# Last convolution taps moved into the first attention, top-k rounds placed between index sums, GpSimd held back behind ropes, fewer idle matmuls

## The reference

```
first_block:  x += 0.5*swiglu(rms_norm(x))                      # ffn0
              q, k, v, u, mq = rms_norm(x) @ w_in               # mixer A
              y = [sliding_window_attention(q,k,v,sinks),       # 8 heads, window 128
                   silu(layer_norm(causal_conv31(glu(u)))),     # 256 channels, 31 taps
                   memory_cross_attention(mq, mem)]             # 4 heads, 256 keys
              x += y @ w_out;  x += 0.5*swiglu(rms_norm(x))     # ffn1
second_block: mod = silu(c) @ ada_w + ada_b                     # shifts, scales, gates
  mixer B:    q, k, v, qi, ki, wi = h @ w_in
              score = sum over 8 index heads of relu(qi.ki)*wi  # causal
              keep the 128 highest scores of each query (top-k)
              o = softmax over the kept keys, 16 heads; x += g1*(o @ w_out)
              x += g2*swiglu(h)                                 # ffn2
  mixer C:    (b * causal_conv3(c*u)) @ w_out, then ffn3
```

## Time and profile before

| | us |
|---|---|
| runs of the kernel | 2164.49, 2162.81, 2172.12 (median 2164.49) |
| the profiled execution | 2165.37, of which the span from first to last instruction is 2163.4 |
| PE busy, PE weight loads | 2135.3, 1758.0 |
| DVE busy, ACT busy, POOL busy | 1211.7, 783.2, 233.8 |
| mean granted TensorE clock | 0.994 of full |

### The profile page before, as it was taken

The page is one execution under the profiler, slowest core; times in us unless marked ns, Lnnn a source line. Parts: engine busy times, 40 slices in busy tenths (PEclk is TensorE's granted clock), DMA queues, the critical chain, the costliest instruction groups (busy, mean ns, idle before and its releaser), DMA issues.

```text
span 2163.4 us, 28943 instructions
## 1 busy us (share of the span) xinstructions
PE 2135.3 (99%) x10238; PEld 1758.0 (81%) x10238; DVE 1211.7 (56%) x1760; ACT 783.2 (36%) x1081; POOL 233.8 (11%) x237
## 2 busy tenths in 40 slices
PE   9999999999999999999989999999999999999999
PEld 8888888877888888877767888888888878888887
DVE  7555444886566554465796575554456456333333
ACT  6222333547442223334355342223333234222222
POOL 0000201650200030014300200000000000000000
PEclk9999999999999999999989999999999999999999
DMA  5555333320345542323300245542332222222232
GB/s 190 183 185 184 104 95 109 124 82 2 107 156 184 187 136 83 93 93 113 107 21 1 85 139 185 185 155 74 101 117 90 95 88 89 96 97 97 78 99 85
DMA packets 75733, 242.96 MB, mean 112 GB/s; under 512 B 9328, under 2 KB 9584, under 8 KB 75536
## 3 DMA queue, kind: packets, MB, share of 16 engines
q1 hardware_dynamic: 61376, 189.61, 26.9%
q0 software_dynamic: 14288, 52.44, 7.8%
HBM read 235.65 MB, written 2.10 MB: 110 GB/s over the span
## 4 chain that ended last, share of the span: by engine, by line
PE 89%; DVE 8%; ACT 1%; issue 1%; DMA 0%; SPq 0%; ACTq 0%; DVEq 0%
PE ps L675 27%; PE ps L677 27%; PE ps L676 27%; PE ps L993 2%; DVE ps L1931 2%; PE ps L951 1%; PE ps L972 1%; PE ps L770 1%; DVE tmp L1604 1%; DVE score L2032 1%; DVE top L2030 1%; PE ps L954 1%; PE ps L1119 0%; DVE w_lo L1561 0%; DVE ropB L1805 0%
## 5 line engine op out<-in xcount | busy, mean ns | idle before, releaser
L675 PE MATMUL ps<-h_hi,w_hi 128*128 128x512 f32 x1888 | 743.3, 394 | 1.3 <-DVE h_lo L1871 0.9
L677 PE MATMUL ps<-h_hi,w_lo 128*128 128x512 f32 x1888 | 735.8, 390 | 0.0
L676 PE MATMUL ps<-h_lo,w_hi 128*128 128x512 f32 x1888 | 735.3, 389 | 0.0
L1561 DVE TENSOR_TENSOR w_lo<-w_raw,w_hi 128x1024 fp32r<-128x1024 f32 x336 | 412.8, 1230 | 433.3 <-ACT w_hi L1202 418.3
L1202 ACT ACTIVATE w_hi<-w_raw 128x1024 fp32r<-128x1024 f32 x383 | 402.3, 1051 | 247.0 <-PE ps L677 245.5
L675 PEld LDWEIGHTS ps<-h_hi,w_hi 128*128 128x128 f32 x1888 | 354.0, 187 | 81.0 <-issue 7.1
L677 PEld LDWEIGHTS ps<-h_hi,w_lo 128*128 128x128 f32 x1888 | 353.8, 187 | 76.2
L676 PEld LDWEIGHTS ps<-h_lo,w_hi 128*128 128x128 f32 x1888 | 354.1, 188 | 72.7 <-issue 0.2
L675 PE MATMUL ps<-hid_hi,w_hi 128*128 128x512 f32 x704 | 273.9, 389 | 0.0
L676 PE MATMUL ps<-hid_lo,w_hi 128*128 128x512 f32 x704 | 273.9, 389 | 0.0
L677 PE MATMUL ps<-hid_hi,w_lo 128*128 128x512 f32 x704 | 273.9, 389 | 0.0
(11 more groups left out here) (304 smaller groups left out, 1749.1 us busy)
## 6 DMA issues: line engine op xcount, KB each, us to landing
ada_raw<-in_ada_w POOLq DMA_DIRECT2D x96, 512.0 KB, 4.3
w_raw<-in_gate SPq DMA_DIRECT2D x88, 512.0 KB, 3.5
w_raw<-in_up SPq DMA_DIRECT2D x88, 512.0 KB, 3.5
w_raw<-in_down SPq DMA_DIRECT2D x64, 384.0 KB, 3.0
w_raw<-in_down SPq DMA_DIRECT2D x64, 320.0 KB, 2.8
w_raw<-in_w_mix_c SPq DMA_DIRECT2D x24, 512.0 KB, 3.5
w_raw<-in_w_mix_b SPq DMA_DIRECT2D x17, 512.0 KB, 3.5
w_raw<-in_w_mix SPq DMA_DIRECT2D x16, 512.0 KB, 3.5
```

The source lines that it names most:

```text
L675: pe.matmul(dest, s_hi, m_hi, start=first and n == 0, stop=False)
L676: pe.matmul(dest, s_hi, m_lo, start=False, stop=False)
L677: mm = pe.matmul(dest, s_lo, m_hi, start=False, stop=last and n == len(pairs) - 1)
L1561: dve.tensor_tensor(chunk(w_lo, slot, WT), chunk(w_raw, slot, WT), f32(chunk(w_hi, slot, WT)), ALU.subtract).then_inc(w_lo_done, 1)
```

## The change

In mixer A, 11 of the 62 taps go from steps 13 to 15 into turns 1 to 11 of the first attention, one a turn, all of half 1. Tap 19 of that half now writes `conv` and taps 20 to 30 read and write it in SBUF; the score of pair 1, which uses banks 2 and 3, waits for tap 19. The total moves to u = 13, the two centrings to u = 15 and 16, the squares to 16 and 17, the sums to u = 20 to 23. In mixer B each step has rounds ahead of its index sums and between their two halves, 33 in all; the 15 left come at u = 7 to 21, and qB7 is roped at u = 1. GpSimd's split of job 9 waits for the rope of qi3, of job 10 and 11 for index sums, and of jobs 15 to 20 for the ropes of qB0 to qB5. The idle matmuls are 4 in the first attention and 5 in the second.

```diff
--- before.py
+++ after.py
@@ -424,9 +424,12 @@
             TOPS += [(b, "tri")] + [(b, r, s) for r in range(ROUNDS) for s in ("max", "take")] + [(b, "mask")]
         top = Marks(sem("top"), TOPS)
         ROUND_LIST = [(b, r) for b in range(1, TT) for r in range(ROUNDS)]
-        TOPS_AT = {9: 3, 10: 3, 11: 2, 12: 3, 13: 3, 14: 3, 15: 3, 16: 3, 17: 2}
-        TOP_EARLY = sum(TOPS_AT.values())
-        TAPS_AT = {2: 3, 3: 3, 4: 6, 5: 6, 6: 5, 7: 6, 8: 3, 9: 5, 10: 5, 11: 5, 12: 4, 13: 4, 14: 4, 15: 3}
+        TOPS_AT = {8: (0, 1), 9: (4, 1), 10: (5, 2), 11: (4, 1), 12: (0, 2), 13: (3, 0), 14: (3, 0), 15: (3, 0), 16: (3, 0),
+                   17: (1, 0)}
+        TOP_EARLY = sum(before + between for before, between in TOPS_AT.values())
+        TAPS_AT = {2: 3, 3: 3, 4: 6, 5: 6, 6: 5, 7: 6, 8: 3, 9: 5, 10: 5, 11: 5, 12: 4}
+        LATE_TAPS = 2 * CONV_A - sum(TAPS_AT.values())
+        LEAVES_BANK = [CONV_A - 1, CONV_A - LATE_TAPS - 1]
 
         def index_slot(m, part):
 
@@ -660,6 +663,14 @@
             pool.wait_ge(x_done, 32)
             pool.dma_start(matsB[:, :], A["mats"]).then_inc(stage_in, 16)
             for j in range(LEAD, len(TILES_B) + KC):
+                if j == 9:
+                    after(pool, h_roped, "qi3")
+                if j == 10:
+                    after(pool, i_sum, (1, 5))
+                if j == 11:
+                    after(pool, i_sum, (2, 1))
+                if 15 <= j <= 20:
+                    after(pool, h_roped, f"qB{j - 15}")
                 split(first_job["mixB"] + j)
             after(pool, h_roped, "qB7")
             ada_steps(2)
@@ -924,12 +935,12 @@
                                        start=True, stop=True)
                 mm.then_inc(h_spread.at(t), 1)
 
-            def attention(pairs, score, turn, values, sums, std):
+            def attention(pairs, score, turn, values, sums, std, beside_exp):
                 for u in range(len(pairs) + 5):
                     if u == 2:
                         after(pe, a_misc, std)
                         after(pe, u_score, pairs[1])
-                        idle(10)
+                        idle(beside_exp)
                     if u < len(pairs):
                         score(pairs[u])
                     if 2 <= u < len(pairs) + 2:
@@ -1041,13 +1052,13 @@
             betweenA(len(TILES_A), 0)
 
             def sumsA(u):
-                if u == 2:
+                if u == LATE_TAPS + 2:
                     after(pe, d_conv, (CONV_A - 1, 1))
                     for c in range(2):
                         mm = pe.matmul(bank(5), ones[:, :], chunk(conv, c), start=c == 0, stop=c == 1)
                     mm.then_inc(p_misc.at("conv_total"), 1)
-                if 5 <= u < 5 + TT:
-                    b = u - 5
+                if LATE_TAPS + 9 <= u < LATE_TAPS + 9 + TT:
+                    b = u - LATE_TAPS - 9
                     if b == 0:
                         after(pe, a_misc, "conv_sq1")
                     for c in range(2):
@@ -1069,7 +1080,7 @@
             def scoreA(pair):
                 kind, j, b = pair
                 if PAIRS_A.index(pair) == 1:
-                    after(pe, d_conv, (CONV_A - 1, 1))
+                    after(pe, d_conv, (LEAVES_BANK[1], 1))
                 if b == 0 and kind == "win":
                     after(pe, h_roped, f"qA{j}")
                 if b == 0 and kind == "mem":
@@ -1094,7 +1105,7 @@
                                                                (2 * (j * MT + q) + half + 1) * HV] for q in range(MT)])
 
             take(first_job["outA"] + 1)
-            attention(PAIRS_A, scoreA, lambda pair: pair_turn(pair, pA, M, matsA), valuesA, sumsA, "stdA")
+            attention(PAIRS_A, scoreA, lambda pair: pair_turn(pair, pA, M, matsA), valuesA, sumsA, "stdA", 4)
             out_chunk("outA", 6, oA_hi, oA_lo, ("a", 9))
             out_chunk("outA", 7, oA_hi, oA_lo, ("a", 11))
             out_chunk("outA", 4, oA_hi, oA_lo, "c0")
@@ -1170,7 +1181,7 @@
             take(first_job["outB"] + 1)
             after(pe, h_scaled, "qB7")
             after(pe, i_relu, IDX[-1])
-            attention(PAIRS_B, scoreB, lambda pair: pair_turn(pair, pB, T, matsB), valuesB, sumsB, "stdB")
+            attention(PAIRS_B, scoreB, lambda pair: pair_turn(pair, pB, T, matsB), valuesB, sumsB, "stdB", 5)
             out_chunk("outB", 6, oB_hi, oB_lo, ("b", 15))
             out_chunk("outB", 7, oB_hi, oB_lo, ("b", 15), last=True)
             out_rest("outB", 4, oB_hi, oB_lo)
@@ -1459,8 +1470,8 @@
 
             def conv_part(u):
 
-                if u == 4:
-                    for c in range(2):
+                if u in (LATE_TAPS + 5, LATE_TAPS + 6):
+                    for c in [u - LATE_TAPS - 5]:
                         after(act, d_misc, f"ctr{c}")
                         act.activation(chunk(hsA, c), chunk(conv, c), ACT.Square).then_inc(a_misc.at(f"conv_sq{c}"), 1)
                 if u == 25:
@@ -1928,7 +1939,8 @@
                     dve.tensor_scalar(bank(2 + c), src, w, col("b_dw", c), ALU.mult, ALU.add).then_inc(d_conv.at((t, c)), 1)
                 else:
                     after(dve, d_conv, (t - 1, c))
-                    dve.scalar_tensor_tensor(chunk(conv, c) if t == CONV_A - 1 else bank(2 + c), src, w, bank(2 + c),
+                    dve.scalar_tensor_tensor(chunk(conv, c) if t >= LEAVES_BANK[c] else bank(2 + c), src, w,
+                                             chunk(conv, c) if t > LEAVES_BANK[c] else bank(2 + c),
                                              ALU.mult, ALU.add).then_inc(d_conv.at((t, c)), 1)
 
             done = 0
@@ -1974,9 +1986,11 @@
                     query_inverse("A", 8 * len(QUERIES[0]), qscA, qnsA)
 
             def conv_part(u):
-                if u == 3:
+                if 1 <= u <= LATE_TAPS:
+                    conv_tap(CONV_A - LATE_TAPS - 1 + u, 1)
+                if u in (LATE_TAPS + 4, LATE_TAPS + 5):
                     after(dve, p_misc, "conv_total")
-                    for c in range(2):
+                    for c in [u - LATE_TAPS - 4]:
                         dve.scalar_tensor_tensor(chunk(conv, c), bank(5), -1.0 / (2 * P), chunk(conv, c), ALU.mult,
                                                  ALU.add).then_inc(d_misc.at(f"ctr{c}"), 1)
                 if u == 26:
@@ -2053,19 +2067,21 @@
                               chunk({"kB": kB, "qB": qB, "qi": qi}[r[:2]], int(r[2])))
                 if m == 4:
                     head_rstd("ki")
-                for b, r in ROUND_LIST[done:done + TOPS_AT.get(m, 0)]:
-                    take_top(b, r)
-                done += TOPS_AT.get(m, 0)
-                for b, h in index_step(m):
-                    index_sum(b, h)
+                for part in range(2):
+                    rounds = TOPS_AT.get(m, (0, 0))[part]
+                    for b, r in ROUND_LIST[done:done + rounds]:
+                        take_top(b, r)
+                    done += rounds
+                    for b, h in index_slot(m, part):
+                        index_sum(b, h)
                 if n in h_normed.value and m > 3:
                     head_norm(n, straight(n))
 
             def topB(u):
-                for b, r in ROUND_LIST[TOP_EARLY + u - 1:TOP_EARLY + u] if u >= 1 else []:
+                if u == 1:
+                    head_rope("qB7", ropB, chunk(qB, 7))
+                for b, r in ROUND_LIST[TOP_EARLY + u - 7:TOP_EARLY + u - 6] if u >= 7 else []:
                     take_top(b, r)
-                if u == 3:
-                    head_rope("qB7", ropB, chunk(qB, 7))
 
             query_inverse("B", 8 * len(QUERIES[1]), qscB, qnsB)
             attention(PAIRS_B, qnsB, pTB, T, osbB, topB)
```

## The result

The changed kernel takes 2146.99 us (median of 5 executions, 2144.53 to 2150.99) against 2163.0 us (5 executions, 2161.07 to 2172.12): a ratio of 0.9919, 95% interval 0.9896 to 0.9942. The forecast was 2150.0, within 2144 to 2160. The profiled execution is the one of 2146.99 us; its span is 2145.2 us, 18.2 less than before, where the prediction had 14.5 less.

A forecast was written before the change was run, and what follows sets the result against it. PE bounds the kernel (busy 99%), so gains lie only where it waits, runs unread work or runs at the lower clock. Mixer A -3.5 and mixer B -11.0 give -14.5 us from 2165.4: 2150.9, as median 2150.0, range 2144 to 2160.

The forecast's parts named there:

- The wait for the reciprocal, and the clock behind it: Mixer A ahead of its attention: PE's wait falls 3.1 us to about 1.0, and the clock stays up, -3.4 us.
- The first attention: Mixer A: late taps make DVE the bound from u = 1 to 11, fewer idle passes save 1.5 us; +3.0 us.
- crowding: First attention: 11 taps in DVE's queue make a pair cost 2.5 us where PE needs 2.1; 4.5 us with moved work.
- the sign of being right: First attention, turns 1 to 11: DVE busy over 95%, with PE's short waits on exponentials.
- The rival that taps cost their latency: First attention: each tap counts all of 0.79 us in place of 0.4; +4.3 us, 2154.3 us; chance 0.09.
- Up to the attention of mixer B: Mixer B before pair 0's maximum: holds save 1.2 us at ki and about 2.5 us at the ropes of kB0, qB0, qB2.
- the rival's 10 us: Mixer B: splits only move onto other operations and swaps for qB4 to qB7 come late; +10 us, 2160; chance 0.06.
- The second attention: Mixer B: first eight pairs faster without rounds until u = 7, pair 24's mask wait of 1.9 us gone; 7.3 us saved.
- the 2.0 us for a start at the lower level: Second attention: 2.0 us added for a low-clock start, with only 5 of 10 idle matmuls in a 2.8 us wait.
- The prediction's second way of counting: Mixer B: PE's losses of 19.1 us, of which about 9.9 would remain; with ki's 1.2 it gives -10.4 us.
- a fall as long as the rival's 10 us: Both attentions: the clock falls once more in each, for 10 us, +4.0 and +3.8 us, 2157.8 us; chance 0.18.
- The slower case: Both attentions: the low clock holds through all DVE-bound pairs, +31.5 us, so +17 and 2181 us; chance 0.05.

The follow-up runs named there:

- taps13: The changed kernel with the four taps of step 13 back ahead of the reciprocal, so seven late taps, not eleven: 2151.01 us, ratio 0.9935.
- idle10: The changed kernel with 20 idle passes in each attention, as before, in place of 8 and 10: 2147.64 us, ratio 0.9927.
- b_part: The changed kernel with mixer A as in the kernel before, so only mixer B's part of the change: 2152.14 us, ratio 0.9949.
- idle0: The changed kernel with no idle passes in either attention: 2150.25 us, ratio 0.9920.
- no_hold: The changed kernel without any of GpSimd's nine new waits: 2152.3 us, ratio 0.9945.
- fill: The changed kernel with 7 and 4 unread matmuls ahead of the sums of two later norms: 2146.0 us, ratio 0.9913.
- tune: The changed kernel with a twelfth late tap, the last hold waiting for qB6's rope, and qB7's rope two turns later: 2147.31 us, ratio 0.9914.
- old_rounds: The changed kernel with mixer B's top-k rounds and the rope of qB7 in their old places: 2155.54 us, ratio 0.9948.
- again: The changed kernel itself, run once more unchanged: 2146.32 us, ratio 0.9903.
- hold_q_only: The changed kernel without the three early holds around ki's rope, keeping those for qB0 to qB5: 2152.12 us, ratio 0.9931.

## Why the prediction was right, point by point

**The wait for the reciprocal, and the clock behind it: right.** Predicted -3.1 and -3.4; measured -6.23 together, and taps13, which loses 6.05, splits that into 3.2 and 2.9. The timeline of DVE answers to the earlier trace rows; the reciprocal comes right behind the last of four taps:

```profile
463.36 2.33 DVE L1942 SCALAR_TENSOR_TENSOR ps<-glu,cols,ps 128x512 f32<-128x512 f32 x3
465.73 0.75 DVE L1942 SCALAR_TENSOR_TENSOR conv<-glu,cols,ps 128x512 f32<-128x512 f32 x1
466.39 0.17 DVE L1797 RECIPROCAL hrA<-hrA 128x4 f32<-128x4 f32 x1
```

**The first attention: mechanism right, size wrong.** This is the step that failed most: +3.0 predicted (4.5 of crowding less 1.5 of idle passes), -0.13 measured. The idle passes are worth 1.35 (idle10), so the crowding costs 1.2. DVE does set the pace of turns 1 to 11, as this stretch of its timeline shows, without a gap from one maximum to the next. (Over all these turns it was busy 23.29 of 25.08 us, 93%, where the sign of being right was over 95%.)

```profile
480.16 0.68 DVE L1837 TENSOR_REDUCE small<-ps 128x2 f32<-128x512 f32 x1
480.88 0.16 DVE L1845 TENSOR_TENSOR small<-small,qnsA 128x2 f32<-128x2 f32 x1
...
481.27 0.16 DVE L1849 TENSOR_TENSOR small<-sink,small 128x2 f32<-128x2 f32 x1
481.35 0.74 DVE L1942 SCALAR_TENSOR_TENSOR conv<-glu,cols,conv 128x512 f32<-128x512 f32 x1
482.01 0.42 DVE L1837 TENSOR_REDUCE small<-ps 128x2 f32<-128x256 f32 x1
```

But a tap takes 0.66 us there (481.35 to 482.01), not the 0.79 of eight in a row: 11 x 0.13 = 1.4 us of the 1.7 by which DVE's 26.8 was too much (25.08 measured). And after pair 12 the moved total and sums brought 2.3 us, not 3.9 (77.67 against 75.35 us from there to the end of the projection). From each of them to the start of the next matmul they take 3.6 us; what hid the rest is not shown. The rival that taps cost their latency was wrong in the other direction.

**Up to the attention of mixer B: sum right by luck, shares wrong.** The prediction gave 1.2 to ki and 2.5 to the ropes; the trace gives 0.2 and 3.7, and the two misses cancel. The holds did bring ki's last operations to 0.69 us each, but DVE then waited for the swap of kraw, 2.76 us:

```profile
991.88 0.69 DVE L1818 TENSOR_TENSOR ropB<-pTB,ada_raw 128x512 f32<-128x512 f32 x1 [2.76 <-DMA pTB<-kraw]
992.60 0.69 DVE L1820 TENSOR_TENSOR ki<-ropB 128x512 f32<-128x512 f32 x1
```

That wait was what ended last, and the prediction's sum named only the operations behind it, as if it stayed at the 1.14 us of the kernel before. In three of the ten kernels with the early holds (b_part, idle10, idle0) it did stay at 1.14 or 1.15; there PE's wait for ki is gone and the stage is 83.94 us, the predicted 1.2 less than before. In the other seven it was 2.36 to 2.90. What makes the swap late is open. Over the ten the early holds come to 0.8.

The 3.7 us are not the ropes alone. Before, three rope operations were slow beside a split (1.64, 1.60 and 1.36 us), 2.5 over their 0.69 or 0.68, which is the term of the sum. One is slow after it, the first operation of qB6, beside the split of job 20; it takes 0.85 back:

```profile
1077.70 1.53 DVE L1816 TENSOR_TENSOR ropB<-qnB,ada_raw 128x512 f32<-128x512 f32 x1
```

So the ropes gave 1.7. Another 1.1 came from an operation that the prediction did not price, the addition of the triangular mask to a block's scores. It had run beside the split at 1069.29 of the kernel before; first before, then after:

```profile
1070.65 1.37 DVE L2027 TENSOR_TENSOR score<-score,matsB 128x128 f32<-128x128 f32 x1
```

```profile
1075.98 0.28 DVE L2041 TENSOR_TENSOR score<-score,matsB 128x128 f32<-128x128 f32 x1
```

The last 0.9 lies in the order of the small operations and in short waits, and is not taken apart further.

The swaps were in time: the rope of qB7 waited 0.25 us for its own, in place of the rival's 10 us.

**The second attention: right, but for the low clock.** Turns with a round take 20.99 / 8 = 2.62 us (2.63 predicted), the mask's 1.9 went, and the first eight pairs run as laid out, a little faster. PE's timeline answers to the earlier trace rows:

```profile
1081.71 1.35 PE L713 MATMUL ps<-ones 128*128 128x128 f32 x10
1083.19 0.49 PE L962 MATMUL ps<-kB,qB 64*128 64x128 f32 x4
...
1086.53 0.49 PE L962 MATMUL ps<-kB,qB 64*128 64x128 f32 x4 [1.10 <-ACT pB L1374]
...
1092.41 0.70 PE L962 MATMUL ps<-kB,qB 64*128 64x256 f32 x4
```

From pair 4 to pair 8 a pair takes 1.47 us (1.6 predicted), and the 2.0 us for a start at the lower level did not come: the ten passes just fill the wait. That is most of the 2.4 us by which this stage beat its term. It is in part luck: b_part, no_hold, idle10, fill and tune, with the same rounds and at least as many passes, did spend 3.4 us at the lower level there. The term was too large even so, since in b_part and fill that cost 0.2 to 0.3 us. The prediction's second way of counting left out one of the three stretches of the earlier trace rows: 1.7 + 1.7 + 5.1 make 8.5 us for the clock, and its -10.4 should have been -12.1; mixer B measured -13.6.

**The rivals.** The clock fell in neither attention of the profiled execution. That it can fall is not a matter of the code there alone: idle0, old_rounds and taps13 each spent 13 to 21 us at the lower level at the start of the second attention, and the five kernels just named 3.4 us. taps13 has exactly the mixer B of the changed kernel, so a fall as long as the rival's 10 us can happen with it. One of the eleven executions of the changed kernel, 2150.99 us at 0.995, may have been such a case; it has no profile. The slower case, a low level all through the DVE-bound turns, showed nowhere; turns 1 to 11 of the first attention were at 1.00 in every profile. In all the span fell by 3.7 us more than predicted: the first attention gave 3.1 more, the ropes 1.2 and the second attention 2.4, ki and the start of mixer A 1.3 less, and 1.75 came back outside the mixers. So the measured time fell close to the forecast while single terms missed by 1 to 3 us in both directions.

## What to carry to other kernels

Price work that is moved into a DVE-bound turn by its pitch (from its start to the start of the next operation) among other operations, and check with the turn's full list of operations what the turn takes; a row of equal, dependent operations overstated it here (0.79 us for 0.66). Read a wait's whole chain before you book its removal: with the slow operation mended, the DMA ahead of it still decided. When two edits shorten the same stage, look at which engine ends it after the first; the second may find nothing left to gain. Fill a wait of PE with unread passes up to its end and no further: without any the clock may fall (idle0), and each one too many costs its full time where the other engine sets the pace (idle10). Do not count on passes to hold the clock, and do not credit an edit with a vanished fall of the clock before several executions without the edit have been seen.

## What the runs showed that was not expected

The granted clock differs between executions of one kernel, and with it the time: the kernel before ran at mean clocks of 0.986 to 0.996 with spans of 2176.6 to 2157.9 us, the changed one at 0.995 to 0.999 with 2149.1 to 2142.6. So part of the 16 us is the clock. That the new order leaves PE fewer places where it falls is the likely reason, not a shown one.

A wait of 0.77 us was followed by 3.4 us at the lower level in again (1227 us) and not in hold_q_only, one of 0.95 us (ahead of the first attention) in none of the profiles that have it. So the length of a wait alone does not tell; the prediction had taken it to.

The same instructions of mixer B kept 1.00 at the start of the second attention in again, spent 3.4 us at the lower level in b_part, where mixer A took 6 us longer, and 20.5 us in taps13, where it took 5 us longer. fill, with mixer A as in again, had 3.4 us too, so the later start is not what decides it. What does is open.
